# Reordering the loads of a gated merge: gate logits ahead of the output panels, and the first group's sigmoid moved into mixer C's end

## The chip, the cores and the metric

The kernel runs on one core of one Trainium2 chip. Its time is the device time of one execution, in microseconds (us); for a kernel the median of several executions is given. TensorE (PE) multiplies, VectorE (DVE) and ScalarE (ACT) work on tiles, GpSimd (POOL) issues gathers, and SyncE (SP) issues most of the other DMAs. The engines run side by side and wait for one another on semaphores. TensorE has two clock levels, 2.4 GHz and 1.2 GHz; the profile's granted clock shows them as 1.00 and 0.50.

## The reference, cut to what matters

One inference step of one decoder layer for 512 prompt tokens and 8 sample tokens, all in float32. Four token mixers A to D run on slices of one input projection, and their results are merged under sigmoid gates:

```
gates = sigmoid(h @ w_merge_gate + b_merge_gate)        # 520 x 4096
ga, gb, gc, gd = split(gates, 4)
merged = ga*(oa @ w_branch_a) + gb*(ob @ w_branch_b) + gc*(oc @ w_branch_c) + gd*(od @ w_branch_d)
x = x + g1 * (merged @ w_out)                           # then norm, router, 64 experts (top 8), shared expert
```

## The kernel before, in words

One program lays all five queues out by hand. The order of work is: input projection and mixers (to about 710 us), merge, output projection with router and shared expert, then the 64 experts in blocks, then the final sum.

**Gate logits.** While the mixers run, TensorE fills its gaps with a fixed list of small jobs (`FILL`): among them 64 pieces that compute the gate logits, and late columns of the adaLN modulation (`("ada", 11)` is the last of these). ScalarE evicts each piece with its bias (`evict`, L943) and stores each row pair to DRAM (`gated[j]`, semaphores `gst0`, `gst1`), because the arena has no room for all 32 tiles of 128x520. Five gate pieces (`FILL_END`) stand inside mixer C's end, between its four row blocks.

**The merge** (L2242 on TensorE, L1638 and L1641 on VectorE, L1072 on ScalarE) has 32 steps j, four for each of eight groups k = j // 4. Step j multiplies the transposed mixer outputs `oT` by a panel of a branch weight into a pair of PSUM banks (three row chunks for branch A, k = 0 and 4, two for the others), and VectorE multiplies that by the sigmoid of gate tile j, adds it to `mT` and counts `m_acc`. There are four bank pairs, so TensorE's step j waits for `m_acc` of step j - 4. After step 7 VectorE does `late_modulation` (L1287 to L1289 and L1283). Group k needs three things: its branch panel (`branch_load(k)`, semaphore `w_br`), its four logit tiles back from DRAM (`gate_back(k)`, semaphore `gl_in`), and ScalarE's sigmoid of them in place (`m_sig`). The logit tiles have three places, so `gate_back(k)` for k >= 3 waits for `m_acc` of group k - 3. The output projection starts when `m_acc` is 32; it uses two panels of `w_out`, each 2048 KB.

**SyncE's queue** issues all these loads from one line, L405, in written order, and a wait in it holds everything behind it:

```
branch 0, branch 1, modulation stores, state stores of mixer C
wait gst (all gate logits stored); gate_back(0), gate_back(1), out panel 0
small stores and loads; wait d_o and rows_out; branch 2, branch 3, adaLN biases, norm gain, gate_back(2)
wait oT_ps; x again (2048 KB)
k = 4: branch 4, gate_back(3)
k = 5: branch 5, gate_back(4)
k = 6: branch 6, gate_back(5), [wait br_ps 24: six groups multiplied] out panel 1
k = 7: branch 7, gate_back(6)
gate_back(7), shared expert's weights
```

The wait on `br_ps` 24 is needed because out panel 1 overwrites the branch panels of groups 4 and 5. The logits' places are `HT` (the transposed h, dead after the last gate piece), `HT + 2080` and `T + 4680`.

**Mixer C's end** on ScalarE: copies of the chunk keys (L1039), then `evict(FILL_END[0])`, then per row block a copy of the raw result (L1052), a square root (`c_root`, L1046) and one more eviction. VectorE updates the state and scales the rows between these (L1622 or L1624, then L1602 to L1613).

Of the kernel before, what the change touches and what calls it, by code (L numbers as in the profile page):

```python
# [11 lines left out]
ALU = mybir.AluOpType  # L12
ACT = mybir.ActivationFunctionType
# [5 lines left out]
P = 128  # L19
# [3 lines left out]
NT = SEQ // P  # L23
NS = 8
TILES = NT + 1
TOK = SEQ + NS
AH, BH, CH, DG, HD = 6, 4, 4, 4, 64
# [24 lines left out]

SEMS = """p_ps p_ready c_prep bs_pe bs_act bs_dve s_act s_soft s_trans const_ready params_in x_in c_in bada_in silu_c     dense_out dense_evac
mod_gain bc_ps rstd_sqrt h_row h_ps hT_evac hro0 hro1
w_in0 w_in1 w_br0 w_br1 w_br2 w_br3 gp0 gp1 fl_ps fl_evac gst0 gst1 modd_out w_late gl_in0 gl_in1 gl_in2 br_ps qk_sum qk_sqrt qk_norm t_ps t_evac t_act rows_out
a_s a_nm a_exp a_p a_pt a_ptc a_pv a_o
b_z b_l b_lk b_after b_sum b_e b_a b_pv b_o
    kvk_used kvv_used qd_ready qb_ps as_used       as_ov as_pv as_o
# [59 lines left out]
FILL = [("gate", u) for u in range(GATE_C)]  # L118
# [21 lines left out]
def trunk(nc, A, O):  # L140
# [15 lines left out]
    with ExitStack() as ctx:  # L156
# [5 lines left out]
        def view(off, dims, parts=P, dt=F32):  # L162
            n = 1
            for d in dims:
                n *= d
            ap = arena[0:parts, off:off + n]
            if dt is not F32:
                ap = ap.bitcast(dt)
            names = "abcd"[:len(dims)]
            if len(dims) > 1:  # L170
                kw = {names[i]: dims[i] for i in range(1, len(dims))}
                ap = ap.rearrange(f"p ({' '.join(names)}) -> p {' '.join(names)}", **kw)
            return ap
# [131 lines left out]
        c_qd = view(W + 8328, [2, NS, NS])  # L305
        cs_lf, cs_k = view(W + 8720, [2, NS]), view(W + 8736, [2, NS])
        c_ss = view(W + 8488, [TILES, CH])
        c_vdiag = view(T + 2048, [2, NS, HD], NS)
        c_S0 = view(T + 3072, [NS, 2, HD])
        c_new = view(T + 4096, [NS, 2, HD])  # L310
        c_vb = [view(AM + 512 * hp, [NS, HD]) for hp in range(2)]
        c_sq = view(W + 4096, [CH, HD])
        OT_BANK = [2, 3, 6]
# [4 lines left out]
        mT = view(W, [KC, TOK])  # L318
        gate_rows = [[view(at + TOK * i, [TOK]) for i in range(2)] for at in (W + 7680, MOD)]
        late_raw = mod_sb[:, 2, :]  # L320
        gate_group = [view(at, [4, TOK]) for at in (HT, HT + 2080, T + 4680)]
        tmp_m = [view(W + 4160 + 520 * i, [TOK]) for i in range(2)]

        acc = [view(at, [D]) for at in (PV, PV + D, PV + 2 * D, PV + 3 * D, HT + 5 * D)]
# [78 lines left out]
        def _(sp):  # L403
            def load(dst, src, s):
                sp.dma_start(dst, src).then_inc(sem[s], 16)  # L405
# [4 lines left out]
            def panel_load(kind, g):  # L410
                i = at_of[(kind, g)]
                half = panels[i][2]
                s = f"w_in{half}"
                if same_half[i]:
                    before, g0, _ = panels[same_half[i][-1]]
                    sp.wait_ge(sem["dense_out"], used_at[before](g0))
                dst = panel[half]
                if kind == "in":
                    w = min(PANEL, IN_W - g * PANEL)
                    load(dst[:, :, 0:w], w_panel("w_in", g * PANEL, w), s)  # L420
                elif kind == "out":
                    if g == 0:
                        sp.wait_ge(sem["fl_ps"], len(FILL))
                    else:
                        sp.wait_ge(sem["br_ps"], 24)
                    load(dst, w_panel("w_out", g * PANEL, PANEL), s)
# [18 lines left out]
            def branch_load(k):  # L445
                half, br = k // NB, k % NB
                if k == 0:
                    sp.wait_ge(sem["fl_ps"], FILL_AT[("ada", 11)] + 1)
                if k >= 4:

                    sp.wait_ge(sem["br_ps"], 4 * (k - 4) + 4)
                name = "w_branch_" + "abcd"[br]
                load(branch_panel[k % 4][:, 0:BR_K[br], :], w_panel(name, half * PANEL, PANEL), f"w_br{k % 4}")

            def gate_back(k):
                if k >= 3:

                    sp.wait_ge(sem["m_acc"], 4 * (k - 3) + 4)
                load(gate_group[k % 3], gated[4 * k:4 * k + 4].rearrange("m p n -> p m n"), f"gl_in{k % 3}")

            def ada_load(n):

# [63 lines left out]
                    gate_load(15)  # L526
            branch_load(0)
            branch_load(1)
            sp.wait_ge(sem["fl_evac"], FILL_AT[("ada", 11)] + 1)
            for j in range(4):  # L530
                load(modd.rearrange("r (g j x) -> j r g x", j=4, x=P)[j], late_raw[32 * j:32 * j + 9, :].rearrange("p (g x) -> p g x", x=P), "modd_out")
# [4 lines left out]
            sp.wait_ge(sem["c_s"], NT)  # L536
            for two in range(2):
                load(O["hgrn_p"].rearrange("(c two) k v -> two k c v", two=2)[two], c_S[two * HD:two * HD + HD, :, :], "hg_out")
            for i in range(2):
                sp.wait_ge(sem[f"gst{i}"], 256)  # L540
            gate_back(0)
            gate_back(1)
            panel_load("out", 0)
            sp.wait_ge(sem["d_gelu"], 1)
            sp.dma_start(O["sgu_v_s"], pv[0:NS, NT, 1408:1664]).then_inc(sem["rows_out"], 16)
            sp.wait_ge(sem["modd_out"], 96)
            load(mod_sb[0:9, 2, :], modd[:, 0:D], "bada_in")
            load(mod_sb[0:9, 0:2, :].rearrange("p a b -> p (a b)"), modd[:, D:3 * D], "bada_in")
            load(gate2, modd[:, 3 * D:4 * D], "bada_in")

# [3 lines left out]
            branch_load(3)  # L554
            load(bada2.rearrange("p a b -> p (a b)"), A["b_ada"][0, 2 * D:6 * D].partition_broadcast(9), "bada_in")
            load(g9b, A["norm2_g"][0].partition_broadcast(9), "bada_in")
            sp.wait_ge(sem["s0_in"], 16 * 6)
            gate_back(2)

            sp.wait_ge(sem["oT_ps"], 13)  # L560
            load(xr[:, 0:NT, :], A["x_prompt"][0].rearrange("(t p) d -> p t d", p=P), "x2_in")
            load(xr[0:NS, NT, :], A["x_sample"][:, 0, :], "x2_in")
            for k in range(4, 8):
                branch_load(k)
                gate_back(k - 1)
                if k == 6:
                    panel_load("out", 1)
            gate_back(7)
            sp.wait_ge(sem["mod_gain"], 7)
            load(w_shared_gu[:, :, 0:ED], w_panel("w_sh_gate", 0, ED), "w_late")  # L570
            load(w_shared_gu[:, :, ED:2 * ED], w_panel("w_sh_up", 0, ED), "w_late")
# [249 lines left out]
        def _(act):  # L821
# [215 lines left out]
            for j in range(2):  # L1037
                act.wait_ge(sem["c_kt"], j + 1)
                act.copy(c_krow[:, 4 * j:4 * j + 4, :], bank[6 + j][:, :].rearrange("p (c n) -> p c n", n=P)).then_inc(sem["c_ktc"], 1)  # L1039
            evict(FILL_END[0])  # L1040

            def c_root(k, t):
# [24 lines left out]
            act.copy(oT[:, 0:5, SEQ:TOK], os_T).then_inc(sem["oT_evac"], 1)  # L1067


            for k in range(8):  # L1070
                act.wait_ge(sem[f"gl_in{k % 3}"], 16 * (LATE_HALVES[k % 3] + k // 3 + 1))
                fn(gate_group[k % 3], gate_group[k % 3], ACT.Sigmoid).then_inc(sem["m_sig"], 1)  # L1072
            def spread(k, first, b):
                act.wait_ge(sem["g_ps"], k)
# [125 lines left out]
        def _(dve):  # L1200
# [323 lines left out]

            def c_values(hp):
                for two in range(2):
                    last = tt_(c_vdiag[:, two, :, :], vc[:, 2 * hp + two:2 * hp + two + 1, :].to_broadcast([NS, NS, HD]), d8.unsqueeze(2).to_broadcast([NS, NS, HD]), ALU.mult)
                last.then_inc(sem["c_vd"], 1)

            def c_state(hp):  # L1530
# [344 lines left out]
        def _(pe):  # L1875
# [126 lines left out]
            def fill(f):  # L2002

                kind, u = FILL[f]
                o = bank[f % 2]
                if f >= 2:
                    pe.wait_ge(sem["fl_evac"], f - 1)
                if kind == "new":
                    pe.wait_ge(sem["c_vd"], u + 1)
                    for two in range(2):  # L2010
                        last = mm(o[two * HD:two * HD + HD, :], ones[0:NS, 0:HD], c_vdiag[:, two, :, :].rearrange("p b v -> p (b v)"), start=True, stop=True)
                elif kind == "read":
                    pe.wait_ge(sem["c_new"], 2)
                    for h in range(CH):
                        j = h % 2 * 32
                        for b in range(NS):
                            last = mm(o[j:j + NS, h * HD:(h + 1) * HD], c_qd[head(h), h // 2, b, :], c_new[head(h), b, h // 2, :], start=(b == 0), stop=(b == NS - 1))
                elif kind == "mix":
                    pe.wait_ge(sem["d_gelu"], 1)
                    for g in (2 * u, 2 * u + 1):  # L2020
                        last = mm(o[:, 256 * (g % 2):256 * (g % 2) + 256], sgu_wt[:, g, :], pv[:, 0:NT, 1408 + g * HD:1472 + g * HD], start=True, stop=True)
                elif kind == "gate":
                    q, ms = u // 4, slice(u // 2 % 2 * P, u // 2 % 2 * P + P)
                    pe.wait_ge(sem[f"gp{q % 2}"], 16 * (q // 2 + 1))
                    for c in range(KC):
                        last = mm(o[:, 0:HALF], gate_place(q)[:, c, ms], hT[:, c, row_half[u % 2]], start=(c == 0), stop=(c == KC - 1))  # L2026
                else:
                    for c in range(KC):
                        n = 2 * (u - 4) + c // 4
                        if c % 4 == 0:  # L2030
                            pe.wait_ge(sem[f"gl_in{n % 3}"], 16 * (n // 3 + 1))
                        for j in range(4):
                            last = mm(o[32 * j:32 * j + 9, 0:P], cT[:, c, :], late_half[n % 3][:, c % 4, j * P:(j + 1) * P], start=(c == 0), stop=(c == KC - 1))
                last.then_inc(sem["fl_ps"], 1)
# [452 lines left out]
```

## Time and profile before

| | |
|---|---|
| median of 3 runs | 1643.7 us (1642.86 to 1645.55) |
| the profiled execution, its own time | 1647.0 us |
| its span in the trace | 1645.2 us |
| mean granted clock of TensorE | 0.959 |
| TensorE busy in the span | 1529.7 us |

The span is what the trace covers, from the first instruction to the last; the execution's own time has 1.8 us more around it. All times below are from this one execution, counted from the span's start. "Idle before" is the time in which the engine waited ahead of an instruction, and the arrow names what ended it; where a wait has several semaphores, the profile names the one that came last by its records.

### The profile page before, as it was taken

The numbers are of one execution on the slowest core, as the hardware profiler recorded it, in microseconds if no ns is written. First come the engines' busy times: TensorE is split into PE (matmuls) and PEld (weight loads), VectorE is DVE, ScalarE is ACT, GpSimd is POOL, SyncE is SP. The second block draws the span as 40 slices with busy tenths as digits, with TensorE's granted clock in tenths as the row PEclk, the third lists the DMA queues.
The fourth block names the chain that finished last, engine by engine and source line by source line (L and its number), as shares of the span: only waits on it lengthen the run. The fifth ranks groups of instructions, "written<-read, shape, count | busy, mean of one in ns | idle before, by whom it ended". The sixth has DMA issues, their size and how long they took to land.

```text
span 1645.2 us, 21310 instructions
## 1 busy us (share of the span) xinstructions
PE 1529.7 (93%) x8211; PEld 822.7 (50%) x8211; DVE 649.4 (39%) x1115; ACT 355.9 (22%) x675; POOL 498.0 (30%) x545
## 2 busy tenths in 40 slices
PE   4999998999999889997899979999999998999988
PEld 4444455777788647886455533333333333333323
DVE  4799972333312666345557611111111111111126
ACT  3101133422542223231233111111111111111120
POOL 3122101211000013000000355656666666666400
PEclk9999999999999789899899989999999999999969
DMA  9787644877322568466311699999899899979676
GB/s 314 269 323 273 248 152 169 292 268 264 100 74 82 166 205 302 135 209 231 101 51 52 240 402 418 399 416 412 325 358 409 334 419 397 362 274 416 235 269 267
DMA packets 138471, 437.30 MB, mean 266 GB/s; under 512 B 31575, under 2 KB 59595, under 8 KB 103535
## 3 DMA queue, kind: packets, MB, share of 16 engines
q0 software_dynamic: 65088, 303.29, 47.8%
q1 hardware_dynamic: 68112, 122.39, 21.8%
q10 hardware_dynamic: 5200, 10.65, 1.7%
q8 instruction: 49, 0.80, 0.2%
q14 instruction: 22, 0.17, 0.0%
HBM read 507.52 MB, written 45.61 MB: 336 GB/s over the span
## 4 chain that ended last, share of the span: by engine, by line
PE 81%; DMA 7%; DVE 3%; issue 3%; ACT 2%; another core or an unknown queue 2%; POOL 1%; SPq 0%; POOLq 0%; ACTq 0%; DVEq 0%
PE bank L2385 18%; PE bank L2026 14%; PE bank L1937 11%; PE bank L2410 9%; PE bank L2254 4%; PE bank L2242 3%; PE bank L2371 3%; PE bank L2449 2%; DMA arena<-in_w_exp_up_dram,arena 2%; PE bank L2059 2%; DMA arena<-in_w_in_dram 1%; DMA arena<-expert_rows 1%; PE bank L2044 1%; PE bank L2395 1%
## 5 line engine op out<-in xcount | busy, mean ns | idle before, releaser
L2385 PE MATMUL bank<-arena 128*64 128x512 f32 x1536 | 345.7, 601 | 8.2 <-issue 4.2
L2026 PE MATMUL bank<-arena 128*128 128x260 f32 x1024 | 240.9, 391 | 0.0
L2385 PEld LDWEIGHTS bank<-arena 128*64 128x64 f32 x1536 | 106.9, 136 | 211.4 <-issue 206.4
L2026 PEld LDWEIGHTS bank<-arena 128*128 128x128 f32 x1024 | 194.3, 194 | 34.8 <-ACT arena L943 2.7
L2410 PE MATMUL bank<-arena 128*64 128x512 f32 x768 | 184.5, 605 | 7.1 <-issue 6.4
L1937 PE MATMUL bank<-arena 128*128 128x512 f32 (+1 forms) x448 | 189.8, 579 | 0.0
L1803 DVE TENSOR_TENSOR arena<-arena,bank 128x256 f32<-128x256 f32 x48 | 20.3, 423 | 353.6 <-ACT arena L1140 270.6
L1937 PEld LDWEIGHTS bank<-arena 128*128 128x128 f32 x448 | 83.5, 189 | 97.8 <-issue 90.4
L713 POOL DMA_INDIRECT arena<-in_w_exp_gate_dram,arena x96 | 95.7, 997 | 71.0 <-issue 61.0
L713 POOL DMA_INDIRECT arena<-in_w_exp_down_dram,arena x96 | 96.1, 1001 | 29.8 <-issue 28.6
L2410 PEld LDWEIGHTS bank<-arena 128*64 128x64 f32 x768 | 53.5, 137 | 102.9 <-issue 96.9
L713 POOL DMA_INDIRECT arena<-in_w_exp_up_dram,arena x96 | 95.8, 998 | 29.2 <-issue 29.2
L703 POOL TENSOR_TENSOR arena<-arena 128x1024 f32<-128x1024 f32 x8 | 25.6, 3203 | 242.8 <-ACT arena L1033 242.7
L1819 DVE COPY arena<-bank 128x512 f32<-128x512 f32 x48 | 33.2, 693 | 165.4 <-PE bank L2410 100.0
L1140 ACT ACTIVATE arena<-bank 128x256 f32<-128x256 f32 x48 | 18.5, 385 | 319.3 <-PE bank L2385 216.9
L691 POOL DMA_INDIRECT arena<-in_cache_sb_v_dram,arena x32 | 30.0, 937 | 180.3 <-PE bank L2059 105.5
L2242 PE MATMUL bank<-arena 128*128 128x260 f32 x288 | 65.8, 390 | 13.2 <-DVE arena L1641 12.5
L1337 DVE TENSOR_TENSOR arena<-arena,bank 128x2048 f32<-128x2048 f32 x32 | 73.3, 2290 | 3.5 <-PE bank L1967 2.4
L1339 DVE TENSOR_REDUCE arena<-arena 128x32 f32<-128x2048 f32 x32 | 73.2, 2288 | 1.1
L691 POOL DMA_INDIRECT arena<-in_cache_sb_k_dram,arena x32 | 30.1, 941 | 143.3 <-DVE arena L1337 113.1
L2371 PEld LDWEIGHTS bank<-arena 128*128 128x128 f32 x384 | 47.2, 194 | 47.8 <-issue 40.3
L943 ACT ACTIVATE arena<-bank,arena 128x260 f32<-128x260 f32 x64 | 30.3, 477 | 177.2 <-PE bank L2026 176.8
(435 smaller groups left out, 1799.4 us busy)
## 6 DMA issues: line engine op xcount, KB each, us to landing
arena<-in_w_ada_dram SPq DMA_DIRECT2D x24, 1024.0 KB, 7.7
arena<-in_w_merge_gate_dram SPq DMA_DIRECT2D x16, 1024.0 KB
arena<-expert_rows SPq DMA_DIRECT2D x16, 1024.0 KB, 7.6
arena<-in_w_in_dram SPq DMA_DIRECT2D x6, 2048.0 KB, 14.2
gate_logits<-arena ACTq DMA_DIRECT2D x32, 260.0 KB, 5.9
arena<-gate_logits SPq DMA_DIRECT2D x8, 1040.0 KB, 10.2
arena<-in_cache_swa_k_dram SPq DMA_DIRECT2D x24, 192.0 KB, 5.1
arena<-in_cache_swa_v_dram SPq DMA_DIRECT2D x24, 192.0 KB, 3.5
```

What stands on the lines that cost most here:

```text
L691: pool.indirect_dma_start(out=dst, out_offset=None, in_=src, in_offset=bass.IndirectOffsetOnAxis(ap=idx_kv[:, b, c:c + 1], axis=0)).then_i ...
L713: pool.indirect_dma_start(out=dst, out_offset=None, in_=src, bounds_check=NE * P - 1, oob_is_err=False, in_offset=bass.IndirectOffsetOnAxi ...
L1337: tt_(bs_prod, key_slot[n % 3], q, ALU.mult).then_inc(sem["kvk_used"], 1)
L1339: step(dve.tensor_reduce(bs_z[:, b, 8 * c:8 * c + 8, :], bs_prod.rearrange("p r (h d) -> p r h d", d=HD), AX, ALU.add))
L1819: dve.tensor_copy(ybuf[q][:, 512:1024], bank[6][:, :]).then_inc(sem["y_v"], 1)
L1937: last = mm(bank[k % 2][:, 0:w], hT[:, c, cols(t)], src[:, c, 0:w], start=(c == 0), stop=(c == KC - 1))
L2026: last = mm(o[:, 0:HALF], gate_place(q)[:, c, ms], hT[:, c, row_half[u % 2]], start=(c == 0), stop=(c == KC - 1))
L2242: last = mm(o, w[:, c, ms], oT[:, BR_AT[br] + c, part], start=(c == 0), stop=(c == BR_K[br] - 1))
L2254: last = mm(o[:, :], mT[:, c, cols(t)], src[:, c, :], start=(c == 0), stop=(c == KC - 1))
L2371: ins = tr(bank[c // 4][:, (c % 4) * P:(c % 4 + 1) * P], xg[q].rearrange("p (n c) -> p c n", c=KC)[:, c, :], ident)
L2385: ins = mm(bank[gu_bank[q]][r, :].rearrange("p (g n) -> p g n", g=2), xT[q][:, c, r], wgu[2 * q + lane][:, :, c, :], start=(c == 0), stop= ...
L2410: ins = mm(bank[5 + m][r, :], hmT[q][:, c, r], wdn[2 * q + lane][:, c, m * 512:(m + 1) * 512], start=(c == 0), stop=(c == 1))
```

## The change

- `gate_back(0)` is issued right behind branch panel 1, ahead of the modulation stores. It waits for `c_q` 8 and, as all of the first three groups now do, only for its own four tiles to be stored (`gst` 32 (k + 1)), not for all 32.
- Its place is `T + 4680`, free there: the group places rotate, and mixer C's sample tiles move (`c_vdiag` out of T, `c_S0` and `c_new` down by 1024 words). It has a semaphore of its own, `gl_first`.
- ScalarE does the sigmoid of group 0 in mixer C's end, ahead of `evict(FILL_END[0])`; the loop of sigmoids at the merge starts at group 1.
- `gate_back(1)` and `gate_back(2)` wait for the last fill job (`HT` is dead then) and are issued one behind the other. The wait for all gate stores goes behind the first modulation load.
- The second load of x moves from ahead of branch 4 to behind `gate_back(4)`.
- Out panel 0 moves from ahead of the merge to the place where out panel 1 was (k = 6, behind `gate_back(5)`), and out panel 1, with its wait on `br_ps` 24, moves behind `gate_back(7)`.

```diff
-        c_vdiag = view(T + 2048, [2, NS, HD], NS)
-        c_S0 = view(T + 3072, [NS, 2, HD])
-        c_new = view(T + 4096, [NS, 2, HD])
+        c_vdiag = [view(at, [NS, HD], NS) for at in (MOD + 2 * TOK, BS_Z + 1152)]
+        c_S0 = view(T + 2048, [NS, 2, HD])
+        c_new = view(T + 3072, [NS, 2, HD])
...
-        gate_group = [view(at, [4, TOK]) for at in (HT, HT + 2080, T + 4680)]
+        gate_group = [view(at, [4, TOK]) for at in (T + 4680, HT, HT + 2080)]
...
             def gate_back(k):
-                if k >= 3:
-
+
+                if k < 3:
+                    for i in range(2):
+                        sp.wait_ge(sem[f"gst{i}"], 32 * (k + 1))
+                else:
                     sp.wait_ge(sem["m_acc"], 4 * (k - 3) + 4)
-                load(gate_group[k % 3], gated[4 * k:4 * k + 4].rearrange("m p n -> p m n"), f"gl_in{k % 3}")
+                load(gate_group[k % 3], gated[4 * k:4 * k + 4].rearrange("m p n -> p m n"), f"gl_in{k % 3}" if k else "gl_first")
...
             branch_load(0)
             branch_load(1)
+            sp.wait_ge(sem["c_q"], 8)
+            gate_back(0)
             sp.wait_ge(sem["fl_evac"], FILL_AT[("ada", 11)] + 1)
...
-            for i in range(2):
-                sp.wait_ge(sem[f"gst{i}"], 256)
-            gate_back(0)
+            sp.wait_ge(sem["fl_ps"], len(FILL))
             gate_back(1)
-            panel_load("out", 0)
+            gate_back(2)
             sp.wait_ge(sem["d_gelu"], 1)
             sp.dma_start(O["sgu_v_s"], pv[0:NS, NT, 1408:1664]).then_inc(sem["rows_out"], 16)
             sp.wait_ge(sem["modd_out"], 96)
             load(mod_sb[0:9, 2, :], modd[:, 0:D], "bada_in")
+            for i in range(2):
+                sp.wait_ge(sem[f"gst{i}"], 256)
...
-            sp.wait_ge(sem["s0_in"], 16 * 6)
-            gate_back(2)
-
-            sp.wait_ge(sem["oT_ps"], 13)
-            load(xr[:, 0:NT, :], A["x_prompt"][0].rearrange("(t p) d -> p t d", p=P), "x2_in")
-            load(xr[0:NS, NT, :], A["x_sample"][:, 0, :], "x2_in")
             for k in range(4, 8):
                 branch_load(k)
                 gate_back(k - 1)
+                if k == 5:
+                    sp.wait_ge(sem["oT_ps"], 13)
+                    load(xr[:, 0:NT, :], A["x_prompt"][0].rearrange("(t p) d -> p t d", p=P), "x2_in")
+                    load(xr[0:NS, NT, :], A["x_sample"][:, 0, :], "x2_in")
                 if k == 6:
-                    panel_load("out", 1)
+                    panel_load("out", 0)
             gate_back(7)
+            panel_load("out", 1)
...
                 act.copy(c_krow[:, 4 * j:4 * j + 4, :], bank[6 + j][:, :].rearrange("p (c n) -> p c n", n=P)).then_inc(sem["c_ktc"], 1)
+            act.wait_ge(sem["gl_first"], 16)
+            fn(gate_group[0], gate_group[0], ACT.Sigmoid).then_inc(sem["m_sig"], 1)
             evict(FILL_END[0])
...
-            for k in range(8):
-                act.wait_ge(sem[f"gl_in{k % 3}"], 16 * (LATE_HALVES[k % 3] + k // 3 + 1))
+            for k in range(1, 8):
+                act.wait_ge(sem[f"gl_in{k % 3}"], 16 * (LATE_HALVES[k % 3] + (k // 3 + 1 if k % 3 else k // 3)))
                 fn(gate_group[k % 3], gate_group[k % 3], ACT.Sigmoid).then_inc(sem["m_sig"], 1)
```

## Rows read from the trace of the kernel before

**Rows 1.** The page: busy time by engine, and the last chain's shares.

```profile
PE 1529.7 (93%) x8211; PEld 822.7 (50%) x8211; DVE 649.4 (39%) x1115; ACT 355.9 (22%) x675; POOL 498.0 (30%) x545
...
PE 81%; DMA 7%; DVE 3%; issue 3%; ACT 2%; another core or an unknown queue 2%; POOL 1%; SPq 0%; POOLq 0%; ACTq 0%; DVEq 0%
```

**Rows 2.** Waits of PE, 714 to 798 us: total, times, longest.

```profile
PE bank L2242 <- DVE arena L1641: 12.5, 3, 8.9
```

**Rows 3.** Timeline, PE, the merge: start, length, what, [idle before <- releaser].

```profile
716.25 24.82 PE L2242 MATMUL bank<-arena 128*128 128x260 f32 x112 [0.66 <-ACT arena L1067]
742.98 7.25 PE L2242 MATMUL bank<-arena 128*128 128x260 f32 x32 [1.91 <-DVE arena L1641]
751.96 24.79 PE L2242 MATMUL bank<-arena 128*128 128x260 f32 x112 [1.72 <-DVE arena L1641]
785.61 8.99 PE L2242 MATMUL bank<-arena 128*128 128x260 f32 x32 [8.87 <-DVE arena L1641]
796.24 3.68 PE L2256 MATMUL bank<-arena 128*8 128x128 f32 x128 [1.64 <-issue]
```

**Rows 4.** Timeline, ACT: the sigmoids of groups 3 and 6.

```profile
748.28 1.94 ACT L1072 ACTIVATE arena<-arena 128x2080 f32<-128x2080 f32 x1 [8.65 <-DMA arena<-gate_logits]
...
781.94 1.94 ACT L1072 ACTIVATE arena<-arena 128x2080 f32<-128x2080 f32 x1 [23.59 <-DMA arena<-gate_logits]
```

**Rows 5.** Timeline, DVE: late modulation starts, step 11 ends, step 12 starts.

```profile
735.63 1.22 DVE L1287 TENSOR_TENSOR arena<-arena 9x1024 f32<-9x1024 f32 x1
...
746.36 0.70 DVE L1641 TENSOR_TENSOR arena<-arena 128x520 f32<-128x520 f32 x1
750.31 0.76 DVE L1638 TENSOR_TENSOR arena<-arena,bank 128x260 f32<-128x260 f32 x2 [3.25 <-PE bank L2242]
```

**Rows 6.** Timeline, SP's queue: when loads are issued.

```profile
712.09 0.93 SPq L405 DMA_DIRECT2D arena<-gate_logits  x2
...
730.39 1.43 SPq L405 DMA_DIRECT2D arena<-gate_logits  x1
...
769.81 0.37 SPq L405 DMA_DIRECT2D arena<-in_w_out_dram  x1
...
770.84 1.78 SPq L405 DMA_DIRECT2D arena<-gate_logits  x2
```

**Rows 7.** DMA issues of 671.0, 712.1, 713.1, 730.4, 770.8: KB, us to landing.

```profile
arena<-in_w_branch_b_dram SPq DMA_DIRECT2D x1, 512.0 KB, 5.5
arena<-gate_logits SPq DMA_DIRECT2D x1, 1040.0 KB, 5.4
arena<-in_w_out_dram SPq DMA_DIRECT2D x1, 2048.0 KB, 15.0
arena<-gate_logits SPq DMA_DIRECT2D x1, 1040.0 KB, 17.9
arena<-gate_logits SPq DMA_DIRECT2D x1, 1040.0 KB, 11.1
```

**Rows 8.** Windows: busy per engine, granted clock, DMA share, GB/s.

```profile
752.00:776.80 24.80, 24.74 (x112) 21.01 (x112) 12.84 (x29) 3.88 (x2) 0.00 (x0) 1.00 0.37 133
778.95:789.07 10.12, 3.46 (x8) 2.79 (x9) 4.97 (x12) 3.88 (x2) 0.00 (x0) 0.50 1.07 367
802.90:809.40 6.50, 6.50 (x9) 2.19 (x8) 3.00 (x5) 3.59 (x7) 0.00 (x0) 0.50 0.00 0
```

**Rows 9.** Timeline, mixer C's end: SP's queue, ACT and DVE.

```profile
671.00 0.49 SPq L405 DMA_DIRECT2D arena<-in_w_branch_b_dram  x1
...
678.04 0.59 ACT L1039 COPY arena<-bank 128x512 f32<-128x512 f32 x1 [0.27 <-PE bank L2190]
682.55 0.48 ACT L943 ACTIVATE arena<-bank,arena 128x260 f32<-128x260 f32 x1 [3.92 <-PE bank L2026]
...
683.88 1.28 ACT L1046 ACT_TABLE_LOAD   x1
...
690.78 0.47 DVE L1624 SCALAR_TENSOR_TENSOR arena<-arena,bank 128x64 f32<-128x64 f32 x2 [3.69 <-PE bank L2209]
```

**Rows 10.** Timeline, POOL: the first load of expert weights.

```profile
919.19 1.06 POOL L713 DMA_INDIRECT arena<-in_w_exp_gate_dram,arena  x1 [31.20 <-issue]
```

More of the change, by code:

```diff
@@ L54 @@
 mod_gain bc_ps rstd_sqrt h_row h_ps hT_evac hro0 hro1
-w_in0 w_in1 w_br0 w_br1 w_br2 w_br3 gp0 gp1 fl_ps fl_evac gst0 gst1 modd_out w_late gl_in0 gl_in1 gl_in2 br_ps qk_sum qk_sqrt qk_norm t_ps t_evac t_act rows_out
+w_in0 w_in1 w_br0 w_br1 w_br2 w_br3 gp0 gp1 fl_ps fl_evac gst0 gst1 modd_out w_late gl_in0 gl_in1 gl_in2 gl_first br_ps qk_sum qk_sqrt qk_norm t_ps t_evac t_act rows_out
 a_s a_nm a_exp a_p a_pt a_ptc a_pv a_o
@@ L1526, in c_values @@
                 for two in range(2):
-                    last = tt_(c_vdiag[:, two, :, :], vc[:, 2 * hp + two:2 * hp + two + 1, :].to_broadcast([NS, NS, HD]), d8.unsqueeze(2).to_broadcast([NS, NS, HD]), ALU.mult)
+                    last = tt_(c_vdiag[two], vc[:, 2 * hp + two:2 * hp + two + 1, :].to_broadcast([NS, NS, HD]), d8.unsqueeze(2).to_broadcast([NS, NS, HD]), ALU.mult)
                 last.then_inc(sem["c_vd"], 1)
@@ L2010, in fill @@
                     for two in range(2):
-                        last = mm(o[two * HD:two * HD + HD, :], ones[0:NS, 0:HD], c_vdiag[:, two, :, :].rearrange("p b v -> p (b v)"), start=True, stop=True)
+                        last = mm(o[two * HD:two * HD + HD, :], ones[0:NS, 0:HD], c_vdiag[two].rearrange("p b v -> p (b v)"), start=True, stop=True)
                 elif kind == "read":
```

## The prediction, made before the changed kernel was built

> **What bounds the kernel now.** I read the page first: TensorE is busy 93% of the span and carries 81% of the chain that ended last [rows 1]. So time is saved only where TensorE waits or runs at its low clock. The list of waits, cut to the merge, shows one pair of names, 12.5 us in 3 waits [rows 2]; the timeline of TensorE gives them one by one: 1.91 us ahead of step 12, 1.72 us ahead of step 16, 8.87 us ahead of step 28 [rows 3]. (One merge matmul takes 24.82 / 112 = 0.222 us by its records [rows 3]; groups 0 and 4 have 48 records, the others 32, so 716.25 + 112 x 0.222 is the end of group 2, and the 112 records from 751.96 are groups 4, 5 and 6.) All three name VectorE's L1641, the `m_acc` count, so the next question is what VectorE waited for.
>
> The large one: step 28 needs step 24's eviction, that needs the sigmoid of group 6, and ScalarE did it at 781.94 to 783.88 after 23.59 us of waiting for the logits [rows 4]. SyncE issued that load at 770.84, right behind out panel 1 at 769.81, 11.1 us before it landed [rows 6, 7]. Its own condition (`m_acc` 16) was true at about 756 (four evictions of 0.76 + 0.70 us from 750.31 [rows 5]). It stood behind the wait on `br_ps` 24, which comes true only when TensorE has finished group 5, one group (7 us) before VectorE needs the logits, and then shared the DMA with 2048 KB. The wait at 751.96 is the same in small: step 16 needs step 12's eviction, which began at 750.31, when the sigmoid of group 3 ended (748.28 + 1.94 = 750.22) [rows 4, 5]. The profile names TensorE as the releaser of that eviction, but TensorE's step 12 had ended by 744.8; the logits were the late input, 17.9 us in flight behind out panel 0 and x [rows 6, 7]. The 1.91 us wait is another matter: VectorE does late modulation from 735.63, and step 8's eviction comes behind it [rows 5].
>
> **The part that pays.** Three terms.
> (a) 8.87 us: out panel 1 and its wait go behind `gate_back(7)`, so nothing with that condition stands ahead of branch 7 or logits 6 and 7.
> (b) 1.74 us: behind the idle time the granted clock is 0.50 from 778.95 to 789.07 [rows 8], so group 7 takes 8.99 us where group 3, with as many records, takes 7.25 [rows 3].
> (c) 1.72 us: with x and out panel 0 out of its way, group 3's load lands early.
> Sum 12.3 us.
>
> **What is late next, with the new order.** Group 3's load is issued at about 727.9 (its `m_acc` 4). In flight it takes between 5.4 us (an empty queue) and 17.9 us (the longest seen) [rows 7]; I take a value near 5.4, because the queue ahead of it holds only branch panels. Even at 17.9 it lands at 745.8, the sigmoid ends at 747.7, and VectorE, busy with step 11 until 747.06 [rows 5], evicts step 12 by 749.2; TensorE asks for it at 750.23. So (c) holds at both ends. Step 16 then starts at 750.23, group 6 ends at 775.0 and group 7 at 782.3.
> Group 6's load: `m_acc` 16 is reached when VectorE has caught up, 747.06 + 4 x 1.46 = 752.9. Ahead of it since 747.1 stand logits 5, out panel 0 and branch 7; with it 4.75 MB, at 367 GB/s [rows 8] 12.9 us, so it lands at about 760. At 17.9 us in flight it lands at 770.8, and step 24 is evicted by 774.2, still before TensorE wants step 28 at 775.0. (a) is safe at both ends.
> Group 7's load: `m_acc` 20 at about 762.4; 5.4 to 11.1 us bring it in by 773.5, its sigmoid by 775.4, and step 28's product is ready at 776.8. At 17.9 us the sigmoid ends at 782.2 and four evictions at 788.1 instead of 783.9: 4.2 us lost, the upper bound of this cost.
> Out panel 1 is issued at 768.0 (end of group 5). 15.0 us [rows 7] give 783.0; the first use of this panel is at about 785.7. Out panel 0 and x have over 15 us to spare. Branch 7, issued at 750.4, has 24 us.
> What stays: the 1.91 us (late modulation is untouched: its start is paced by TensorE's step 7) and the 1.64 us between the last matmul of the merge and 796.24 [rows 3], which is the last eviction. So the output projection starts at about 783.9 instead of 796.2.
>
> **The first group's sigmoid.** At the merge it removes 1.94 us of ScalarE, which nothing waits for: TensorE's first steps have free banks. Its cost is in mixer C's end. On SyncE's queue one more issue stands ahead of ten stores, 0.5 to 1.4 us [rows 6, 9], hidden: the last of them to be waited for is needed at 710. The load is issued at about 671.5 behind two branch panels; branch 1 lands at 676.5 [rows 7], 1040 KB more take 2.9 us, so 679.4. ScalarE is free at 678.6, and has nothing else until 682.55 [rows 9]. It now loads the sigmoid table (1.28 us, as the table load at 683.88 [rows 9], which it needs as before) and does 1.94 us [rows 4]: ready at 681.9. If late, it first eats the 3.69 us that VectorE has to spare before 690.78 [rows 9]. Bounds: nothing lost while the sigmoid ends before 682.55 + 3.69; at 17.9 us in flight (landing 689.4, sigmoid done 691.3) it is 8.8 us late and the loss at most 8.8 - 3.7 = 5.1 us. I take nothing, since only 1280 KB stand ahead. Removing the sigmoid from the merge gains nothing either.
> The Trainium skill, ScalarE: Activation LUTs, section What ACT_TABLE_LOAD costs, speaks against this step: a switch of table costs a load of about 1283 ns and a drain of about 1380 ns. The load agrees with the 1.28 us of the row. By the page's full 2.66 us the sigmoid would end at 683.2, 0.7 us behind the eviction's start; the sum would be 12.3 us by either, but the cover is thinner.
>
> **Moved tiles** (`c_vdiag`, `c_S0`, `c_new`) cost nothing: same shapes on the same engines. `gate_back(1)` and `(2)` leave at about 709.5 and 710 instead of 712.09 and 728.55; the small store behind them now has two groups ahead and not a third load of 2048 KB, so branches 2 and 3 are issued near 719 instead of 726.81, and are used at 734.
>
> **Behind the merge** everything is released by computed data: the expert weights' first gather at 919.19 [rows 10] follows the router. No transfer has an absolute time, so the gain passes to the end.
>
> **Rivals.**
> 1. More: behind the merge the clock is low twice for 6.50 us with TensorE at work, from 802.90 and from 823.60 [rows 8], 3.25 us lost each time. They follow matmuls with few rows or columns, not the idle time, so I keep them. If both were an after-effect of the idle stretch, the gain is 12.3 + 6.5 = 18.8 us, 1624.9. The Trainium skill, TensorE: Matmul & The Clock Gate, section What's actually happening, says that the gate's view of activity isn't tied to the kernel's work; by it, low stretches may begin at other points once work is shifted, in either direction. No trace here shows that yet.
> 2. Less: a load turns late. Group 7 late costs up to 4.2 us, C's end up to 5.1: gains of 8.1 or 7.2 us, 3.0 with both; 1636 for one, 1640.7 for both. For it speaks the 17.9 us, against it that only that load stood behind 2048 KB and more.
> 3. The change doesn't do what it says: the wait on group 6 only takes another name (branch 7's panel, say). Against it: its condition, `br_ps` 16, is true at 750.2. Then only (c) is won: 1642.0, within 0.2%.
> 4. Slower: the new wait for `gl_first` stands ahead of ScalarE's evictions and copies in mixer C, which release TensorE. It is on time up to a landing at 682.55 - 1.94 = 680.6, and past another 3.7 us each microsecond costs one. So it outweighs 12.3 us from a landing later than 680.6 + 3.7 + 12.3 = 696.6, 25 us after issue; a 35 us flight loses 22.2 and gives 1653.6. The longest flight seen is 17.9.
>
> **How the numbers follow.** The sum goes against the profiled execution: 1647.0 - 12.3 = 1634.7; that execution was 3.3 us above the median, so the median is 1643.7 - 12.3 = 1631.4. Chances: forecast 0.68 (its own range 1628 to 1635, one low stretch more or less); more 0.11; less 0.12; no effect 0.05; slower 0.04. The range takes in rival 1 and rival 2 in one of its places: 1624 to 1638.5. A measurement can tell about 0.2% (3.3 us) from no change; faster 0.91, same 0.05, slower 0.04.
>
> **What would show it.** Right: no idle time of several us before the last 32 L2242 records, clock 1.00 through the merge, group 6's sigmoid near 762, L2256 near 784, one wait of 1.9 us left at step 12, the sigmoid in C's end done before the eviction. Wrong: idle time of ScalarE at `gl_first` past 684, TensorE waiting in L2242 or on a panel of `w_out`, or the lag lost again behind 800.

## The result

The changed kernel takes 1634.16 us (median of 14 runs) against 1644.05 us for the kernel before (14 runs beside them). The ratio is 0.993, with a 95% interval of 0.9913 to 0.9946, so it is 8.9 to 14.3 us faster (the two medians alone are 9.9 us apart). Taken again later, on a chip where the kernel before is faster, the two took 1612.24 and 1624.22 us, ratio 0.9924 (0.990 to 0.9949). The forecast was 12.3 us: a ratio of 0.9925, a median of 1631.4 us and a range of 1624 to 1638.5. The measured median lies in the range, 2.8 us above the forecast, and the intervals hold the 12.3 us.

Single executions of one kernel differ by more than this gain (1638 to 1655 us for the kernel before), so the traces are compared stage by stage. The stage that the change touches repeats to a tenth of a microsecond.

The timeline of TensorE in the merge, changed kernel (columns as in rows 3; L2242 has become L2248, L2256 has become L2262):

```profile
708.86 24.82 PE L2248 MATMUL bank<-arena 128*128 128x260 f32 x112 [0.66 <-ACT arena L1073]
735.59 38.82 PE L2248 MATMUL bank<-arena 128*128 128x260 f32 x176 [1.92 <-DVE arena L1647]
776.04 3.68 PE L2262 MATMUL bank<-arena 128*8 128x128 f32 x128 [1.64 <-issue]
```

Groups 3 to 7 run in one piece of 176 records where [rows 3] had three pieces with 1.72 and 8.87 us between them. From the merge's first matmul to the output projection's first it takes 776.04 - 708.86 = 67.18 us; before it took 796.24 - 716.25 = 79.99. What is left is what the forecast left: 1.92 us ahead of step 12 and 1.64 us at the end. The window over the 176 records (columns as in rows 8) has the full clock throughout:

```profile
735.60:774.50 38.90, 38.81 (x176) 33.14 (x176) 28.75 (x63) 7.01 (x4) 0.00 (x0) 1.00 0.88 306
```

The page has TensorE at 94% of a span of 1624.4 us and at 83% of the last chain (81% in [rows 1]):

```profile
PE 1520.2 (94%) x8211; PEld 814.6 (50%) x8211; DVE 649.7 (40%) x1115; ACT 356.9 (22%) x676; POOL 501.1 (31%) x545
...
PE 83%; DMA 6%; DVE 3%; ACT 2%; issue 2%; another core or an unknown queue 2%; POOL 1%; SPq 0%; POOLq 0%; ACTq 0%; DVEq 0%
```

The two spans differ by 20.8 us, not by 12.8. The table shows where, for every execution profiled in this study (e1 to e13 are the experiments below). The stages, in us and read from first starts to 0.1 us, are bounded by TensorE's first merge matmul, first L2256 (or its line there), first transpose of the expert stage and first matmul of the final sum. The last column adds up, from one-microsecond windows, how long the clock was at 0.50 in the 140 us behind the merge.

| execution | until merge | merge | output to experts | experts | final sum | low clock behind merge |
|---|---|---|---|---|---|---|
| before | 716.3 | 79.9 | 159.7 | 628.0 | 61.3 | 13.7 |
| changed | 708.9 | 67.1 | 154.4 | 633.3 | 60.7 | 3.4 |
| e1 | 716.1 | 68.5 | 158.4 | 626.4 | 61.4 | 10.3 |
| e2 | 706.8 | 77.8 | 159.4 | 625.3 | 60.7 | 13.6 |
| e3 | 714.3 | 72.6 | 156.8 | 620.8 | 61.2 | 6.8 |
| e4 | 715.9 | 67.2 | 154.6 | 625.6 | 60.9 | 3.4 |
| e5 | 708.4 | 67.2 | 159.0 | 630.3 | 62.0 | 13.6 |
| e6 | 714.3 | 67.1 | 154.6 | 634.3 | 61.6 | 3.4 |
| e7 | 712.7 | 65.0 | 158.1 | 635.7 | 62.0 | 10.2 |
| e8 | 709.5 | 63.3 | 159.5 | 626.7 | 61.9 | 13.7 |
| e10 | 720.8 | 67.2 | 158.8 | 613.8 | 61.8 | 13.6 |
| e13 (e3 again) | 712.5 | 72.7 | 157.6 | 610.9 | 61.0 | 10.3 |
| e11 (changed again) | 714.0 | 67.2 | 155.7 | 612.4 | 60.8 | 6.8 |
| e12 (e8 again) | 710.1 | 63.4 | 156.3 | 611.1 | 61.2 | 6.8 |

Only the merge column follows the kernel. The first column spans 707 to 716 us for kernels with the same work there (720.8 in e10 is that experiment's own wait). In "changed" 7.4 us of the 20.8 are such a difference: ahead of the merge the clock was at 0.50 for 54.6 us in the kernel before and for 37.5 us here, and half of the difference is 8.5 us, an estimate of the same size. The 5.3 us won behind the merge are lost again in the experts. e1 to e4, e5 to e8 and the last four rows ran on three different chips, so the first and fourth columns are compared within such a group only.

### The profile page after: what moved, and what is told of

It reads as the page before. It is cut to its first block, busy times and chain, and to the rows that moved or that the text cites. A ratio compares the mean times of both kernels' runs of the same rounds, so it can differ in the third digit from the quotient of the medians.

```text
span 1624.4 us, 21314 instructions
## 1 busy us (share of the span) xinstructions
PE 1520.2 (94%) x8211; PEld 814.6 (50%) x8211; DVE 649.7 (40%) x1115; ACT 356.9 (22%) x676; POOL 501.1 (31%) x545
## 4 chain that ended last, share of the span: by engine, by line
PE 83%; DMA 6%; DVE 3%; ACT 2%; issue 2%; another core or an unknown queue 2%; POOL 1%; SPq 0%; POOLq 0%; ACTq 0%; DVEq 0%
PE bank L2391 19%; PE bank L2032 13%; PE bank L1943 12%; PE bank L2416 9%; PE bank L2260 4%; PE bank L2248 3%; PE bank L2455 3%; PE bank L2377 3%; DMA arena<-in_w_exp_up_dram,arena 2%; PE bank L2065 2%; DMA arena<-in_w_ada_dram 1%; DMA arena<-in_w_in_dram 1%; PE bank L2050 1%; PE bank L2401 1%
## 5 line engine op out<-in xcount | busy, mean ns | idle before, releaser
L2032 PE MATMUL bank<-arena 128*128 128x260 f32 x1024 | 238.9, 388 | 0.0
L2377 PE MATMUL bank<-arena 128*128 128x128 f32 x384 | 58.1, 291 | 11.2 <-DMA arena<-h_rows,arena 6.5
```

Of the source, the lines that this page charges most:

```text
L2377: ins = tr(bank[c // 4][:, (c % 4) * P:(c % 4 + 1) * P], xg[q].rearrange("p (n c) -> p c n", c=KC)[:, c, :], ident)
```

## The experiments

### Which load held group 6: e1 and e2

e1 is one edit to the kernel before:

```diff
             for k in range(4, 8):
                 branch_load(k)
                 gate_back(k - 1)
-                if k == 6:
-                    panel_load("out", 1)
             gate_back(7)
+            panel_load("out", 1)
```

> One edit to the kernel before: the load of out panel 1, with its wait for br_ps 24, stands behind the loads of logits 6 and 7; out panel 0, x and all gate groups stay where they were, and no sigmoid moves. Theory A (the load and its wait were what made group 6 late): the 8.9 us ahead of step 28 is gone, group 7's 32 records take 7.2 us instead of 9.0 at the full clock, the 1.7 us ahead of step 16 and the 1.9 us ahead of step 12 stay; from the merge's first matmul to the output projection's first it takes 80.0 - 10.6 = 69.4 us, and the time is 10 to 11 us under that of the kernel before. Rival B (the group only takes another late load, panel or logits, because x and out panel 0 are still ahead of everything): 3 us or more of waiting stay ahead of step 28 and the merge takes 73 us or more.

Measured: merge 68.53 us, ratio to the kernel before 0.9941 (0.991 to 0.9972). The timeline of TensorE:

```profile
742.78 7.25 PE L2241 MATMUL bank<-arena 128*128 128x260 f32 x32 [1.91 <-DVE arena L1640]
751.15 31.80 PE L2241 MATMUL bank<-arena 128*128 128x260 f32 x144 [1.11 <-DVE arena L1640]
784.59 3.69 PE L2255 MATMUL bank<-arena 128*8 128x128 f32 x128 [1.64 <-issue]
```

The wait ahead of step 28 is gone and the one ahead of step 16 stays (1.11 us here, 1.72 before). So this edit alone is worth 11.5 of the 12.8 us in the merge, 0.9 more than the 10.6 expected: the shorter wait at step 16 is 0.6 of that. Rival B fell.

e2 is the changed kernel with that part undone:

```diff
                 if k == 6:
                     panel_load("out", 0)
+                    panel_load("out", 1)
             gate_back(7)
-            panel_load("out", 1)
```

> The changed kernel with one part undone: out panel 1, with its wait for br_ps 24, goes back ahead of branch panel 7 and logits 6 and 7. Theory A: 8.5 to 9.5 us of waiting ahead of step 28 are back, the granted clock falls to 0.50 in that wait and group 7 takes 8 to 9.5 us for its records instead of 7.2; the merge takes 67.2 + 10.6 = 77.8 us and the time is about 10.6 us over that of the changed kernel. Rival B (other parts of the change make the gain too): under 5 us.

Measured: merge 77.79 us, ratio to the kernel before 0.9989 (0.9968 to 1.0009), which is no measurable gain. The two lines around step 28:

```profile
733.53 31.80 PE L2248 MATMUL bank<-arena 128*128 128x260 f32 x144 [1.91 <-DVE arena L1647]
774.13 8.83 PE L2248 MATMUL bank<-arena 128*128 128x260 f32 x32 [8.80 <-DVE arena L1647]
```

The 8.80 us and the slow group 7 (8.83 us) are back, as large as in [rows 3], though logits, x and out panel 0 are in their new places. Theory A holds from both sides.

### The wait or the bytes: e3 and e13

```diff
                 if k == 6:
                     panel_load("out", 0)
+                    sp.wait_ge(sem["br_ps"], 24)
             gate_back(7)
```

> The changed kernel with the wait for br_ps 24 alone put back ahead of branch panel 7 and logits 6 and 7; the 2048 KB of out panel 1 stay behind them. It parts the held queue from the bytes ahead. Theory A, by bytes: logits 6 are issued when group 5 is multiplied, with 1552 KB to move at 367 GB/s and about 2 us besides, so they land some 6 us after it, the sigmoid is done 8 us after it and step 24 evicted 9.5 us after it, against 7.1 us that group 6 gives: 2 to 3.5 us of waiting ahead of step 28, the clock stays at 1.00, the merge takes 69.5 to 71 us. Then about 3 of the 8.9 us were the wait and 6 the bytes of out panel 1. Rival B (the wait alone costs it all): 8 us or more ahead of step 28. Rival C (the bytes alone): under 1 us.

> The kernel with the wait for br_ps 24 alone put back, run again. In its first run the 3.5 us wait ahead of step 28 was followed by a clock of 0.50 and group 7 took 8.94 us for its records. Theory A (a wait of that length always drops the clock): the same again, merge 72.6 us. Rival B (whether it drops depends on the execution): the wait is 3.5 us again, but group 7 may take 7.2 us, merge 70.9 us.

Measured: e3's ratio to the kernel before is 0.9948 (0.9924 to 0.9973); e13 is a single execution. TensorE at step 28, e3 and then e13:

```profile
776.36 8.94 PE L2249 MATMUL bank<-arena 128*128 128x260 f32 x32 [3.54 <-DVE arena L1648]
```

```profile
774.64 8.94 PE L2249 MATMUL bank<-arena 128*128 128x260 f32 x32 [3.62 <-DVE arena L1648]
```

The wait alone, with nothing but branch 7 ahead of the logits, costs 3.5 to 3.6 us; the other 5.2 us of 8.80 are the remainder, put down to the 2048 KB ahead: logits 6 were 11.0 us in flight in e2 and 6.4 us in e3. (The bytes without the wait can't be run, since out panel 1 would overwrite branch panels in use.) Theory A was about right on this split (its upper end was 3.5). It was wrong about the clock: in both executions the clock fell just behind this wait, and group 7 took 8.94 us, 1.7 us more than at the full clock. So the merge is 5.5 us longer, not 2 to 4. Windows over the wait and over group 7, e3 and then e13:

```profile
772.80:776.80 4.00, 0.46 (x3) 0.45 (x3) 2.06 (x5) 3.15 (x2) 0.00 (x0) 1.00 1.05 390
776.90:780.20 3.30, 3.30 (x9) 2.63 (x8) 3.22 (x7) 0.51 (x1) 0.00 (x0) 0.50 1.05 384
```

```profile
771.00:774.60 3.60, 0.02 (x1) 0.00 (x0) 1.57 (x4) 2.76 (x2) 0.00 (x0) 1.00 1.05 389
774.60:775.90 1.30, 1.26 (x6) 1.14 (x7) 1.26 (x4) 1.09 (x1) 0.00 (x0) 1.00 1.06 392
776.00:779.30 3.30, 3.30 (x9) 2.50 (x9) 3.20 (x8) 0.00 (x0) 0.00 (x0) 0.50 1.06 375
779.40:783.50 4.10, 4.10 (x19) 3.26 (x18) 3.65 (x8) 0.00 (x0) 0.00 (x0) 1.00 1.09 349
```

The clock is full through the wait, falls 0.5 us (e3) and 1.3 us (e13) behind its end, with TensorE at work again, and is back before the group ends.

### x or out panel 0 in the way of group 3: e5

```diff
+            sp.wait_ge(sem["oT_ps"], 13)
+            load(xr[:, 0:NT, :], A["x_prompt"][0].rearrange("(t p) d -> p t d", p=P), "x2_in")
+            load(xr[0:NS, NT, :], A["x_sample"][:, 0, :], "x2_in")
             for k in range(4, 8):
                 branch_load(k)
                 gate_back(k - 1)
-                if k == 5:
-                    sp.wait_ge(sem["oT_ps"], 13)
...
```

> The changed kernel with the second load of x back ahead of branch panel 4; out panel 0 stays behind logits 5. It parts x from out panel 0 as the cause of the 1.7 us ahead of step 16. Theory A (out panel 0 was the load in the way, since it also held up the store on which branch panels 2 and 3 wait): x is issued at about 4 us behind branch panel 2, the queue has moved it before logits 3 are issued or soon after, step 16 doesn't wait, merge 67.2 us. Rival B (x was in the way): logits 3 are over 12 us in flight and 1 to 1.7 us of waiting ahead of step 16 are back, merge 68.3 to 69 us.

Measured (a single execution): merge 67.19 us; logits 3 were 9.6 us in flight (6.5 us in the changed kernel, 17.9 in [rows 7]), and nothing waits for them. Rival B fell: moving x bought nothing. SyncE's own waits, the kernel before and then the changed one, say how out panel 0 made group 3 late:

```profile
SPq L552 <- DMA out_dram<-arena: 9.2, 1, 9.2
```

```profile
SPq L557 <- DMA out_dram<-arena: 1.6, 1, 1.6
```

This is the wait for a small store written behind out panel 0. Out panel 0's own bytes had landed at 728.1 (713.1 + 15.0 [rows 7]), before logits 3 were issued at 730.39. But branches 2 and 3, logits 2 and x were written behind the wait for that store, so all of them were issued in the 3.6 us ahead of logits 3 (from 726.81 on) and stood in their way. The change also moves logits 2 out of this place; no run parts that from the move of out panel 0, so their shares are not shown.

### The first group's sigmoid: e4, e6, e10

The timeline of ScalarE in mixer C's end, changed kernel:

```profile
672.31 1.28 ACT L1045 ACT_TABLE_LOAD   x1
677.76 1.94 ACT L1045 ACTIVATE arena<-arena 128x2080 f32<-128x2080 f32 x1 [4.17 <-DMA arena<-gate_logits]
679.61 0.46 ACT L947 ACTIVATE arena<-bank,arena 128x260 f32<-128x260 f32 x1
...
680.47 0.44 ACT L1058 COPY arena<-bank 128x128 f32<-128x128 f32 x2 [0.40 <-ACT arena L947]
680.92 1.28 ACT L1052 ACT_TABLE_LOAD   x1
682.22 0.30 ACT L1052 ACTIVATE arena<-arena 8x4 f32<-8x4 f32 x1
```

The timeline of TensorE there, the first and the third fill job:

```profile
671.38 3.67 PE L2032 MATMUL bank<-arena 128*128 128x260 f32 x16
...
683.05 5.35 PE L2032 MATMUL bank<-arena 128*128 128x260 f32 x16
```

The logits came 9.2 us after their issue at 668.55, and the eviction behind the sigmoid began at 679.61, 4.6 us behind the end of its fill job (671.38 + 3.67 = 675.05). In e4 the sigmoid goes back:

```diff
-            act.wait_ge(sem["gl_first"], 16)
-            fn(gate_group[0], gate_group[0], ACT.Sigmoid).then_inc(sem["m_sig"], 1)
             evict(FILL_END[0])
...
+            act.wait_ge(sem["gl_first"], 16)
+            fn(gate_group[0], gate_group[0], ACT.Sigmoid).then_inc(sem["m_sig"], 1)
             for k in range(1, 8):
```

> The changed kernel with the sigmoid of group 0 (and its wait) moved back from mixer C's end to the head of ScalarE's sigmoids at the merge; its logits are still loaded early. Theory A (that sigmoid is on nobody's path in either place): the time is that of the changed kernel within 0.2%, merge 67.2 us, no wait of TensorE between the last modulation fill and the merge changes. Rival B (it frees the start of the merge): 1 to 2 us more in the merge. Rival C (in mixer C's end it costs, since ScalarE waited 4.2 us for the logits there): 1 to 3 us less ahead of the merge.

Measured: merge 67.19 us, ratio to the kernel before 0.9934 (0.9903 to 0.9965). TensorE waits nowhere in mixer C's end, as in the changed kernel. Theory A: the move brings nothing and costs nothing.

e6 and e10 make the logits later, to find what the move could have cost. e6 loads them behind the modulation stores and the sample-state stores; e10 does this load three times there, each waiting for the one before, and the sigmoid waits for the third:

```diff
-            sp.wait_ge(sem["c_q"], 8)
-            gate_back(0)
...
+            sp.wait_ge(sem["c_q"], 8)
+            gate_back(0)
             sp.wait_ge(sem["c_s"], NT)
```

> The changed kernel with the load of logits 0 moved behind the modulation stores and the four sample-state stores, its sigmoid still in mixer C's end. It measures the spare time there. In the changed kernel the sigmoid ended 4.7 us after the fill job whose eviction stands behind it, and TensorE didn't wait. Here the load is issued some 7.5 us later and lands about 8 us later. Theory A (the spare is set by the third fill of mixer C's end, which needs that eviction's bank, some 8 us behind the fill): TensorE waits 1 to 4.5 us at that fill, and the last fill-to-merge stretch is longer by as much; merge 67.2 us. Rival B (the spare was used up at 4.7 us): 6 us or more are lost. Rival C (spare for all of it): no new wait.

> As the run with logits 0 loaded late (behind the state stores), but the load is done three times in a row, each waiting for the one before, and the sigmoid in mixer C's end waits for the third. In that run the eviction behind the sigmoid ended 3.7 us before TensorE's third fill job there began, without a wait. Two more loads of 5.4 us make it 10.8 us later. Theory A (past the spare each microsecond costs one): TensorE waits about 10.8 - 3.7 = 7 us at the third fill job or at the row block behind it, in all 6 to 9 us between the last modulation fill and the merge, and the merge stays at 67.2 us. Rival B (ScalarE's lateness is soaked up further on): under 3 us.

Measured in e6: the sigmoid began at 682.39, the eviction ended at 684.70, and TensorE waited nowhere: rival C. But this run didn't test a larger delay. The clock was at 0.50 from 668 to 678 in it, so the first fill job ended only at 680.51 (675.90 + 4.61), and the eviction began 3.7 us behind that, less than the changed kernel's 4.6. The third fill job, whose bank that eviction frees, began at 688.45. Measured in e10 (a single execution), TensorE's waits from 680 to 700 us and its third fill job:

```profile
PE bank L2035 <- ACT arena L950: 7.6, 1, 7.6
```

```profile
694.28 6.13 PE L2035 MATMUL bank<-arena 128*128 128x260 f32 x16 [7.56 <-ACT arena L950]
```

The sigmoid began at 691.92, 9.5 us later than in e6, and TensorE waited 7.56 us, with the clock at 0.50 from 689 to 699 besides. Theory A holds. The spare runs from the end of the first fill job (678.70) to where the third could have begun (694.28 - 7.56 = 686.72), 8.0 us. The same distance is 683.05 - 675.05 = 8.0 us in the changed kernel and 688.45 - 680.51 = 7.9 in e6. The eviction takes 0.46 us of it, the 4.6 us of the changed kernel lie inside it, and what came later in e10 cost one for one (the eviction ended at 694.22, 7.5 us past 686.72) and the clock on top.

### A shorter merge: e7, e8, e12

```diff
-                if j == 7:
+                if j == 15:
                     late_modulation()
```

> The changed kernel with late modulation moved from behind step 7 to behind step 15. Behind step 7 VectorE is 5.7 us behind and group 2 and 3 evictions have no spare; from step 16 on TensorE needs 2.66 us a step and VectorE 0.76 us. Theory A (the 1.9 us ahead of step 12 is late modulation's place): that wait is gone, no other comes, merge 65.3 us, time 1.9 us under the changed kernel's. Rival B (the wait only moves to step 20): merge 66 to 67.2 us.

Measured: merge 65.04 us; the 1.92 us ahead of step 12 are gone and all 288 records run in one piece. Ratio to the kernel before 0.9883 (0.9843 to 0.9923). Rival B fell.

e8 is e7 with this besides:

```diff
                     for c in range(KC):
+                        if i == 0 and g == 0 and c == KC - 1:
+                            pe.wait_ge(sem["m_acc"], 32)
...
             pe.wait_ge(sem["mod_gain"], 7)
-            pe.wait_ge(sem["m_acc"], 32)
+            pe.wait_ge(sem["m_acc"], 31)
```

> e7 and one thing more: the output projection starts on 31 counted steps, and only its last row chunk of the first bank waits for all 32. The last eviction (0.76 + 0.70 us) then runs beside 1.6 us of matmuls. Theory A: the 1.64 us ahead of the output projection fall to about 0.2, no wait of over 0.5 us comes inside it, the stretch from the merge's first matmul to the output projection's second matmul group is 3.4 us shorter than in the changed kernel, and the time is 3.4 us under the changed kernel's, about 15 us under the kernel before. Rival B (the wait comes back at the last chunk): only 1.9 us.

> The version with late modulation behind step 15 and the output projection started on 31 steps, again, beside the changed kernel on one chip. Merge 63.3 us again, so 3.9 us (0.24%) under the changed kernel's; ratio to the kernel before about 0.9895, median 3 to 5 us under the changed kernel's. Rival: the later stages give it back and both medians are within 1 us.

> The changed kernel itself once more, beside the best version on one chip. Merge 67.2 us as before in every execution. If the stretch from the output projection to the experts is 154.4 us again and no 6.5 us stretch of low clock lies in it, the change also gained there; if it varies between 154 and 160 us, those 5 us were chance. Theory: it varies. Ratio to the kernel before about 0.992.

Measured: merge 63.33 us in both executions, 3.85 us under the changed kernel's. The timeline of TensorE in e8:

```profile
709.50 63.40 PE L2248 MATMUL bank<-arena 128*128 128x260 f32 x288 [0.66 <-ACT arena L1073]
...
772.83 3.81 PE L2264 MATMUL bank<-arena 128*8 128x128 f32 x128
```

The first 128 records of the output projection take 3.81 us instead of 3.68, so the last chunk's wait costs 0.1 us and 3.7 us are won. e8's ratio to the kernel before is 0.9905 (0.9872 to 0.9939): beside each other on one chip e7's median was 1628.96 us (4 runs) and e8's 1629.77 (6 runs), so e8's total doesn't show the 1.7 us that its merge is shorter. On another chip, beside each other, e12 took 1608.23 us (ratio 0.9909, 0.9878 to 0.9939) and the changed kernel 1612.24 us, 4.0 us apart where 3.9 were expected. The intervals of these two ratios overlap, so the shorter merge is shown and the shorter total only made likely. The rival "later stages give it back" expected them within 1 us; it fits less well and isn't ruled out.

## Why the prediction was right, point by point

**Term (a), 8.87 us, and (b), 1.74 us: right in cause and size.** e1 takes them away with one edit, e2 brings back 8.80 us and a group of 8.83 us. The step that blamed both the held queue and the shared DMA is split by e3: 3.5 us by the wait, 5.2 us by the remainder, the bytes.

**Term (c), 1.72 us: right in size, the cause in part.** Group 3's logits landed 6.5 us after their issue. The prediction named x beside out panel 0 as the thing in their way; e5 shows that x alone doesn't bring the wait back. Out panel 0 acted through the store behind it, and the share of logits 2 stays open.

**The sum was 12.3 us, the merge gave 12.8.** Counted from the merge's start, the prediction put the load of logits 3 at 11.65 us, that of logits 6 at 36.65 us and the output projection at 67.65 us. Measured are 720.47 - 708.86 = 11.61, 745.44 - 708.86 = 36.58 and 67.18. The 0.5 us are my adding three rows (7.25 + 24.79 + 7.25 = 39.3); in one piece they are 38.82. The rows of 144 and 176 records give (38.82 - 31.80) / 32 = 0.219 us per record, so 32 records are 7.02 us and a row of its own, 7.25, holds 0.23 us once. One middle value was off at no cost: logits 6 were to land at 760, 43.8 us behind the merge's start, and landed 46.6 us behind it (745.44 + 10.0 - 708.86), well inside the bound of 770.8.

**From the merge to the whole time.** That nothing behind the merge has an absolute time, so that the gain passes to the end, isn't contradicted, but it isn't shown to a microsecond either. Only the merge is measured to 0.1 us; the medians are 9.9 and 12.0 us apart on the two chips, and the intervals reach from 8.3 to 16.2 us.

The SyncE queue of the changed kernel shows the order working; the last line is out panel 1, issued when group 5 was multiplied, and never waited for:

```profile
739.69 0.37 SPq L405 DMA_DIRECT2D arena<-gate_logits  x1
740.15 0.45 SPq L405 DMA_DIRECT2D arena<-in_w_out_dram  x1
742.87 0.37 SPq L405 DMA_DIRECT2D arena<-in_w_branch_d_dram  x1
745.44 9.11 SPq L405 DMA_DIRECT2D arena<-gate_logits  x2
760.45 0.37 SPq L405 DMA_DIRECT2D arena<-in_w_out_dram  x1
```

**The sigmoid in mixer C's end: the cost was right (nothing), the working was not, so this part was luck.** Two sizes were off. I had the sigmoid ready 0.65 us ahead of its eviction; it held it up by 4.6 us, because the load took 9.2 us instead of 7.9 and this execution had the full clock there, so that TensorE came to the fill job sooner. And I put the spare at 3.69 us, VectorE's idle time ahead of its next state update. By that number the changed kernel should have lost 1 us. The true limit is TensorE's third fill job, which needs the bank, 8.0 us behind the end of the first (e10). The eviction behind the sigmoid feeds a bank, not VectorE's update; I read the slack of the wrong consumer. What the Trainium skill says of table switches (ScalarE: Activation LUTs, section What ACT_TABLE_LOAD costs: a load and a drain, 2.66 us together) was no part of this. The rows again show 1.28 us for a load, but not the drain: behind the load of 672.31 ScalarE waited for the logits, so none could be seen, and at the switch back the copy ends at 680.91, the load runs from 680.92 to 682.20 and the square root begins at 682.22. Here the measurement decides: this switch cost 1.3 us, not 2.66.

**Rival 1 (more gain, clock) fell as a cause and stayed as scatter.** e5 and e8 have no long wait in the merge and still have two low stretches of 6.8 us behind it, as the kernel before (13.7 us together in the table); the changed kernel had 3.4 us in one execution and 6.8 in the other. Two windows of e5:

```profile
782.60:789.10 6.50, 6.50 (x8) 2.53 (x8) 3.00 (x5) 3.27 (x6) 0.00 (x0) 0.50 0.03 4
803.00:809.60 6.60, 6.00 (x28) 4.04 (x29) 3.40 (x9) 3.48 (x8) 0.00 (x0) 0.50 0.00 0
```

In the table the stage behind the merge takes about 153 us plus half of its low-clock time, whatever stood ahead of it. This agrees with what the Trainium skill says in TensorE: Matmul & The Clock Gate, section What's actually happening, that the gate's view isn't tied to the work: its place differs from run to run. The prediction was right to leave those 6.5 us (twice 3.25) out of the sum and to put them into the range.

**Rival 2 (a load turns late) and rival 4 (slower).** Group 7's logits were issued at about 754 and landed 5.1 us later. Rival 4's mechanism is real: e10 pays 7.56 us with it. But its price was worked out from the wrong spare, and without the clock, which fell in that wait.

**Rival 3 (the wait takes another name) fell.** TensorE's waits in the changed kernel's merge, 708 to 778 us:

```profile
PE bank L2248 <- DVE arena L1647: 1.9, 1, 1.9
PE bank L2262 <- issue: 1.6, 1, 1.6
PE bank L2248 <- ACT arena L1073: 0.7, 1, 0.7
```

## What to carry to other kernels

In an in-order DMA queue, look for the wait that comes true last and count what is written behind it: here one prefetch, not needed for another 28 us, held three loads that were, and moving that one line was 11.5 of 12.8 us. Follow a wait back twice (the matmul to the eviction, the eviction to the sigmoid, the sigmoid to the load) before you ask what to move. When you spend an engine's idle time, measure the slack at the consumer of the very thing that becomes late, and compare stages rather than single spans when executions scatter by as much as the gain.

## What I had not expected of the hardware

A wait of 3.5 us of TensorE cost 5.5 (72.64 - 67.18): in both executions the clock fell to 0.50 behind it, 0.5 and 1.3 us after TensorE had begun again, where waits of 1.1, 1.7 and 1.9 us in the same merge were never followed by a fall (the 1.9 us wait stands in 11 executions). In the waits of 7.56 to 8.87 us it fell while TensorE still waited. And the same stage with the same work takes 154.4 to 159.7 us from one execution to the next, in step with 3.4 to 13.7 us of low clock. The expert stage does the same work in every kernel here and took 620.8 to 626.4 us on the chip of e1 to e4, 626.7 to 635.7 on that of e5 to e8 and 610.9 to 613.8 on that of the last four; within a group it doesn't follow the merge. Its cause was not looked into and stays open.
